# Two encoder layers on one core: host-laid input and modulation weights, first shift and scale by TensorE tile by tile

## What is computed

```python
def adaln(c, w, b):
    mod = (c @ w + b)[:, None, :]
    shift, scale, gate = jnp.split(mod, 3, axis=-1)
    return shift, scale, gate

for l in range(DEPTH):
    shift, scale, gate = adaln(c, w_ada_mix[l], b_ada_mix[l])
    u = x * (1.0 + scale) + shift
    y = hybrid_mixer(u, w_in[l], ...)
    x = layer_norm(DN_ALPHA * x + (1.0 + gate) * y, ln1_g[l], ln1_b[l])
    shift, scale, gate = adaln(c, w_ada_ffn[l], b_ada_ffn[l])
    u = x * (1.0 + scale) + shift
    y = conv_gated_mlp(u, w_up[l], ...)
    x = layer_norm(DN_ALPHA * x + (1.0 + gate) * y, ln2_g[l], ln2_b[l])
```

## Time and profile before

| what | value |
| --- | --- |
| median of 3 runs | 2102.32 us (2102.18 to 2103.11) |
| the profiled execution's own time | 2101.31 us |
| its span, first to last instruction | 2099.5 us |
| mean granted TensorE clock | 0.997 |
| busy share of PE, DVE, ACT, POOL | 98%, 57%, 49%, 67% |
| HBM read, written | 242.71 MB, 4.26 MB |

### The profile page before, as it was taken

One profiled execution on the slowest core, in us unless ns is written; L12 is line 12 of the kernel. 1 busy time (PEld: TensorE's weight loads), 2 busy tenths in 40 slices (PEclk: granted clock), 3 DMA queues, 4 the chain that ended last, 5 costly groups with the idle time before them and its releaser, 6 DMA issues.

```text
span 2099.5 us, 27374 instructions
## 1 busy us (share of the span) xinstructions
PE 2064.8 (98%) x9619; PEld 1701.8 (81%) x9619; DVE 1191.1 (57%) x1940; ACT 1031.2 (49%) x1845; POOL 1413.6 (67%) x1780
## 2 busy tenths in 40 slices
PE   7999999999999999999999999999999999999997
PEld 6877778787888878888788888888878888888887
DVE  5888888675515554777632645587651455332235
ACT  3585356555516674374643756235562465333332
POOL 4987767755778887875557885564556776545454
PEclk9999999999999999999999999999999999999999
DMA  8644544533434354553233333332323332434332
GB/s 301 157 134 148 161 127 148 162 108 103 121 111 124 107 162 145 141 159 93 76 100 106 111 111 91 101 103 73 100 76 107 88 104 84 128 99 123 94 100 78
DMA packets 421510, 250.07 MB, mean 119 GB/s; under 512 B 48149, under 2 KB 393085, under 8 KB 421373
## 3 DMA queue, kind: packets, MB, share of 16 engines
q1 hardware_dynamic: 420506, 248.03, 39.8%
q10 hardware_dynamic: 867, 0.29, 0.1%
HBM read 242.71 MB, written 4.26 MB: 118 GB/s over the span
## 4 chain that ended last, share of the span: by engine, by line
PE 86%; POOL 5%; ACT 3%; DVE 3%; issue 2%; ACTq 0%; DMA 0%; POOLq 0%; DVEq 0%
PE fg L886 27%; PE fg L888 27%; PE fg L887 27%; POOL w_lo L1932 3%; PE bank_s L984 1%; POOL ada_acc L2003 1%; ACT ada L1324 1%; PE bank_l L915 1%; PE bank_t L993 1%; PE bank_t L1006 1%; DVE bank_c L1539 0%; POOL ssum L2030 0%; POOL u_lo L2012 0%; ACT probs L1291 0%; ACT probs L1283 0%
## 5 line engine op out<-in xcount | busy, mean ns | idle before, releaser
L1932 POOL TENSOR_TENSOR w_lo<-raw,w_hi 128x256 fp32r<-128x256 f32 (+1 forms) x1425 | 1031.3, 755 | 609.8 <-ACT w_hi L1163 608.7
L886 PE MATMUL fg<-u_hi,w_hi 128*128 128x512 f32 x2112 | 834.7, 395 | 6.2 <-DVE u_lo L1519 2.6
L888 PE MATMUL fg<-u_hi,w_lo 128*128 128x512 f32 x2112 | 823.7, 390 | 0.0
L887 PE MATMUL fg<-u_lo,w_hi 128*128 128x512 f32 x2112 | 823.5, 390 | 0.0
L1163 ACT ACTIVATE w_hi<-raw 128x1024 fp32r<-128x1024 f32 (+2 forms) x387 | 375.6, 971 | 385.6 <-PE fg L888 278.4
L886 PEld LDWEIGHTS fg<-u_hi,w_hi 128*128 128x128 f32 x2112 | 397.1, 188 | 102.5 <-issue 14.5
L888 PEld LDWEIGHTS fg<-u_hi,w_lo 128*128 128x128 f32 x2112 | 397.0, 188 | 84.2
L887 PEld LDWEIGHTS fg<-u_lo,w_hi 128*128 128x128 f32 x2112 | 397.4, 188 | 80.1 <-issue 0.5
L1539 DVE SCALAR_TENSOR_TENSOR bank_c<-glu,par,bank_c 128x512 f32<-128x512 f32 x448 | 306.1, 747 | 0.1
L1886 DVE SCALAR_TENSOR_TENSOR x<-fg,mod,x 128x512 f32<-128x512 f32 (+1 forms) x168 | 121.6, 724 | 319.3 <-PE fg L888 319.0
L888 PE MATMUL fg<-h_hi,w_lo 128*128 128x512 f32 (+1 forms) x704 | 269.8, 383 | 0.0
(11 more groups left out here) (272 smaller groups left out, 1860.8 us busy)
## 6 DMA issues: line engine op xcount, KB each, us to landing
raw<-in_w_up_dram SPq DMA_DIRECT2D x176, 512.0 KB, 3.8
ada<-in_w_ada_ffn_dram SPq DMA_DIRECT2D x48, 512.0 KB, 4.4
raw<-in_w_down_dram SPq DMA_DIRECT2D x64, 384.0 KB, 3.5
raw<-in_w_in_dram SPq DMA_DIRECT2D x40, 512.0 KB, 4.0
raw<-in_w_down_dram SPq DMA_DIRECT2D x64, 320.0 KB, 3.1
ada<-in_w_ada_mix_dram SPq DMA_DIRECT2D x32, 512.0 KB, 4.2
raw<-in_w_in_dram SPq DMA_DIRECT2D x32, 256.0 KB, 3.7
raw<-in_w_out_dram SPq DMA_DIRECT2D x32, 256.0 KB, 2.9
```

Of the source, the lines that this page charges most:

```text
L886: pe.matmul(out, hi[:, k, :], rhi, start=k == order[0], stop=False)
L887: pe.matmul(out, hi[:, k, :], rlo, start=False, stop=False)
L888: ins = pe.matmul(out, lo[:, k, :], rhi, start=False, stop=k == order[-1])
L1932: ins = pool.tensor_tensor(lo_of(n)[:, ks, :], raw[n % NRAW][:, ks, :], hi_of(n)[:, ks, :].bitcast(F32), ALU.subtract)
```

## The change

The host now lays out three inputs. x is handed over with features in rows, so SP loads its tiles directly into `x` (`load_x(b, i)`, 512 KB for two tiles of one block). The first modulation weights come as eight blocks of 1 MB (`ada_first`): block k has what shift and scale of feature tile k need, with the output features on the partitions' axis of the weights of a TensorE product. The later modulation weights come transposed (`ada_t`), one output feature a row. The first half of the output is stored with features in rows, and the host turns it.

On TensorE, `first_part(k)` makes shift and scale of tile k with 16 products that have a single moving column (`ccol`). Parts 0 and 1 stand ahead of the first product of slab pair 0 and 1, and part k+1 ahead of the pair's tile k for k = 1 to 6. VectorE adds the constants (`first_fold_in`), ScalarE makes u and `u_hi` (`first_inputs`, for all eight tiles), and VectorE `u_lo` (`first_lo`). The products of the identity (`idle_products`) are gone. The transposes of the convolution taps (`taps_turn`) move behind the pair's last tile. c is spread over the partitions once (`c_rows`, two products of one row by 512 columns).

Later sums: GpSimd multiplies a quarter (128 output features x 1024) by `c_rows` (`ada_weigh`), and ScalarE, one slab later, sums each row by a copy with an accumulated output (steps "ae", `ada_total`); for chunks 8 to 10 VectorE does both in one instruction. The steps "as" and "xt" are gone from all engines, and "tm" is now only a place in SP's list.

```diff
-        if c in ONES_CHUNKS:
-            at(ns[-1] + 2, "as", c)
-        else:
-            put(ns[-1] + 2, "as", c)
+        for part, n in enumerate(ns):
+            if c not in DVE_CHUNKS:
+                at(n + 1, "ae", c, part)
+        if c >= DVE_CHUNKS[0]:
+            used[ns[-1] + 2] += 7
     for n, what, i in ((18, "gate", 0), (47, "gate", 1), (100, "ss", 2), (145, "gate", 2), (165, "ss", 3),
...
+            def load_x(b, i):
+                sp.dma_start(x[:, 2 * i:2 * i + 2, b * T:(b + 1) * T],
+                             a["x"][2 * i * P:2 * (i + 1) * P, b * T:(b + 1) * T].rearrange("(k p) n -> p k n", p=P)).then_inc(in_x[b][i], 16)
             def load_first(k):
-                c0, c1, k0, k1, i, slot = FIRST_PIECES[k]
-                dst = first_ada[i][:].rearrange("p a n -> p (a n)")[:, slot * T:slot * T + (k1 - k0) * (c1 - c0)]
-                sp.dma_start(dst.rearrange("p (k n) -> p k n", n=c1 - c0),
-                             a["w_ada_mix"][0, k0 * P:k1 * P, c0:c1].rearrange("(k p) n -> p k n", p=P)).then_inc(in_first[k], 16)
+                for half in (0, 1):
+                    sp.dma_start(first_ada[k][:, half, :], a["ada_first"][k, half]).then_inc(in_first[k][half], 16)
             def load_ada(m):
-                c, part = CHUNKS_BEFORE + m // QUARTERS, m % QUARTERS
-                l, ffn, j = c // NCHUNK // 2, c // NCHUNK % 2, c % NCHUNK
                 if m >= 2:
-                    sp.wait_ge(ada_add[added(m - 2)[0]], added(m - 2)[1])
-                src = a["w_ada_ffn" if ffn else "w_ada_mix"][l, part * 2 * P:(part + 1) * 2 * P, j * T:(j + 1) * T]
-                sp.dma_start(ada[m % 2][:], src.rearrange("(k p) n -> p k n", p=P)).then_inc(in_ada[m % 2], 16)
+                    sp.wait_ge(*part_done(m - 2))
+                sp.dma_start(ada[m % 2][:], a["ada_t"][m * P:(m + 1) * P, :].rearrange("p (h n) -> p h n", h=2)).then_inc(in_ada[m % 2], 16)
...
+            for k in range(DT):
+                load_first(k)
+                if k < 2:
+                    load_x(0, k)
+                    load_w(k)
+                if k == 3 or k == 5:
+                    load_x(0, (k + 1) // 2)
+            load_rows(rows2, rows3)
             for n in range(2, NRAW):
                 load_w(n)
-            sp.wait_ge(in_first[-1], 16)
-            load_rows(rows2, rows3)
             sp.dma_start(nsink[:], a["sinks"]).then_inc(in_sinks, 16)
-            for t in range(TB, TT):
-                load_x(t)
+            for i in range(DT // 2):
+                load_x(1, i)
...
+            def first_part(k):
+                if k >= 2:
+                    pe.wait_ge(first_fold, 2 * (k - 1))
                 for half in (0, 1):
+                    pe.wait_ge(in_first[k][half], 16)
+                    for d in range(DT):
+                        ins = pe.matmul(bank_c[k % 2][:, half:half + 1], first_ada[k][:, half, d * P:(d + 1) * P], ccol[:, d:d + 1],
+                                        start=(half, d) == (0, 0), stop=(half, d) == (1, DT - 1))
+                ins.then_inc(first_sum, 1)
...
+                if ns[0] == 0:
+                    first_part(1)
...
+                    if ns[0] == 0 and 0 < k < DT - 1:
+                        first_part(k + 1)
...
-                    if ns[0] == 0 and k == DT // 2 - 1:
-                        first_rest()
+                    if ns[0] == 0 and k == DT - 1:
+                        taps_turn()
...
+            for half in (0, 1):
+                pe.matmul((bank_t, bank_s)[half][:], ones_1[0:1, :], c_rows[0:1, half, :], start=True, stop=True).then_inc(set_pe, 1)
             pe.wait_ge(in_const, 16 * IN_CONST)
             for l in range(DEPTH):
                 ins = pe.transpose(fg[1][:, l * P:l * P + N1], rows1[0:N1, l, :], ident[0:N1, 0:N1])
             ins.then_inc(set_pe, 1)
-            first_sums(0)
-            idle_products(12, fg[0])
+            pe.wait_ge(in_ccol, 16)
+            first_part(0)
...
             def first_inputs(k):
-                if k % (DT // 2) == 0:
-                    act.wait_ge(fold_step, FOLDED["half", 2 * k // DT])
-                if k == 0:
-                    for half in (0, 1):
-                        act.wait_ge(x_evac[half], TB)
+                act.wait_ge(first_fold, 2 * k + 2)
+                if k % 2 == 0:
+                    act.wait_ge(in_x[0][k // 2], 16)
+                if k >= 2:
+                    act.wait_ge(ilo[0], k - 1)
+                inputs(tmp[:, k % 2, :], xs(0, k), 0, k, iu)
                 inputs(u_hi[0][:, k, :], xs(0, k), 0, k, ihi)
-                if k < DT // 2:
-                    if k >= 2:
-                        act.wait_ge(ilo, k - 1)
-                    inputs(tmp[:, k % 2, :], xs(0, k), 0, k, iu)
...
-            def ada_scale(c, part):
+            def ada_total(c, part):
                 m = (c - CHUNKS_BEFORE) * QUARTERS + part
-                act.wait_ge(in_ada[m % 2], 16 * (m // 2 + 1))
-                for i in (0, 1):
-                    k = 2 * part + i
-                    act.activation(ada[m % 2][:, i, :], ada[m % 2][:, i, :], ACT.Copy, scale=ccol[:, k:k + 1]).then_inc(ada_mul, 1)
-            def stage(t, src):
+                act.wait_ge(ada_mul, 2 * sum(ada_engine(i) == "act" for i in range(m + 1)))
+                rows = ada[m % 2][:].rearrange("p h n -> p (h n)")
+                act.activation(rows, rows, ACT.Copy, accum_out=total_of(c, part)).then_inc(ada_done["act"], 1)
...
+            for half in (0, 1):
+                act.wait_ge(set_pe, half + 1)
+                act.activation(c_rows[:, half, :], (bank_t, bank_s)[half][:], ACT.Copy).then_inc(set_col, 1)
+            act.wait_ge(set_pe, 3)
             act.activation(par1[:], fg[1][:].rearrange("p (l n) -> p l n", n=P)[:, 0:DEPTH, 0:N1], ACT.Copy).then_inc(set_par, 1)
+            split_hi(0)
             for k in range(DT):
-                if k == DT // 2:
-                    split_hi(2)
                 first_inputs(k)
-            act.wait_ge(set_pe, 4)
+                if k == 0:
+                    split_hi(1)
+            split_hi(2)
+            act.wait_ge(set_pe, 5)
...
+            def first_fold_in(k):
+                dve.wait_ge(first_sum, k + 1)
+                o = OFF["b_ada_mix"] + k
+                sums = bank_c[k % 2]
+                dve.tensor_tensor(bias[:, 0, k:k + 1], sums[:, 0:1], par1[:, 0, o:o + 1], ALU.add).then_inc(first_fold, 1)
+                dve.scalar_tensor_tensor(out=gain[:, 0, k:k + 1], in0=sums[:, 1:2], scalar=1.0, in1=par1[:, 0, o + DT:o + DT + 1],
+                                         op0=ALU.add, op1=ALU.add).then_inc(first_fold, 1)
+            def first_lo(k):
+                dve.wait_ge(ihi, k + 1)
+                dve.wait_ge(iu, k + 1)
+                dve.tensor_tensor(u_lo[0][:, k, :], tmp[:, k % 2, :], u_hi[0][:, k, :].bitcast(F32), ALU.subtract).then_inc(ilo[0], 1)
...
+            def ada_total(c, part):
...
+                rows = ada[m % 2][:].rearrange("p h n -> p (h n)")
+                dve.scalar_tensor_tensor(out=rows, in0=rows, scalar=1.0, in1=c_rows[:].rearrange("p h n -> p (h n)"),
+                                         op0=ALU.mult, op1=ALU.mult, accum_out=total_of(c, part)).then_inc(ada_done["dve"], 1)
...
+            dve.wait_ge(set_par, 1)
+            first_fold_in(0)
+            for k in range(DT):
+                if k + 1 < DT:
+                    first_fold_in(k + 1)
+                first_lo(k)
...
+            def ada_weigh(c, part):
                 m = (c - CHUNKS_BEFORE) * QUARTERS + part
+                pool.wait_ge(in_ada[m % 2], 16 * (m // 2 + 1))
+                pool.wait_ge(set_col, 2)
+                for i in (0, 1):
+                    pool.tensor_tensor(ada[m % 2][:, i, :], ada[m % 2][:, i, :], c_rows[:, i, :], ALU.mult).then_inc(ada_mul, 1)
...
-            for n in range(2):
-                split_lo(n)
-            for k in range(DT // 2):
-                first_lo(k)
+            split_lo(0)
+            split_lo(1)
             angles(0)
             split_lo(2)
-            pool.wait_ge(set_pe, 4)
+            angles(1)
+            pool.wait_ge(set_pe, 5)
...
+def first_rows(w):
+    return np.ascontiguousarray(w[:, :2 * D].reshape(DT, P, 2, DT, P).transpose(3, 2, 1, 0, 4).reshape(DT, 2, P, D))
+def ada_rows(w_mix, w_ffn):
+    rows = np.concatenate([w[l].T for l in range(DEPTH) for w in (w_mix, w_ffn)])
+    return np.ascontiguousarray(rows[CHUNKS_BEFORE * T:])
...
+            "x": np.ascontiguousarray(inputs["x"][0].T), "ada_first": first_rows(inputs["w_ada_mix"][0]),
+            "ccol": np.ascontiguousarray(inputs["c"][0].reshape(DT, P).T),
+            "ada_t": ada_rows(inputs["w_ada_mix"], inputs["w_ada_ffn"])}
     for name in _INS + [n for n in made if n not in _INS]:
```

350 lines of the change are left out of this document (66 added, 284 removed).

## The result

The changed kernel takes **2160.44 us** (median of 4 runs, 2158.70 to 2165.72), beside 2102.72 us for the kernel before in the same session: the ratio is 1.0276, with a 95% interval of 1.0255 to 1.0296. The sign was forecast, the size was not: 2125 us was forecast with a range up to 2142. The profiled execution is the longest of the four, 2165.72 us with a span of 2163.9 us.

A forecast was written before the change was run, and what follows sets the result against it. TensorE was taken as the bound over most of the run, with GpSimd setting the pace from 51.4 to 137 us. Start +32.3 less 10 got gave +22.3 on 2101.31, 2123.6, plus 1.0 for the median: 2125 us, range 2103 to 2142.

The forecast's parts named there:

- 32.3 and -10: Forecast terms: slab 2 starts 32.3 us late, and TensorE's shorter list behind the start gives back 10 us.
- The start's mechanism: Before slab 2: two parts precede the pair, each tile waits for `u_lo`, and single-column records run mostly at low clock.
- the low-clock column of the working: Start worked out at low clock throughout: a period of 10.7 us, slab 2's first products at 98.4 us.
- 8.0 us a period, between 6.1 and 10.7: Start, one part and one tile: most tiles' products bring the clock back for part of the next single-column stretch.
- The rival with low clock throughout: Start: the clock stays low, slab 2 is 49.5 us late, +39.5 us in all, 2142 us; chance 0.20.
- Single columns cost the same at either clock: Start: a part always takes 3.3 us, slab 2 at about 73 us, 2114 us; chance 0.15.
- Got: 10 us: Behind the start: of 16.1 us taken off TensorE's list, 10 us shortens the time, with ends 5 and 16.
- What lies between 51 and 137 us: Second stretch: 4.8 us off TensorE's list is not got, since GpSimd sets the pace there.
- the wait for `kz`: TensorE's wait for VectorE's `kz` ahead of the first attention scores, forecast at 5 to 8 us.
- Cheap edits ... All at nothing: Later sums on ScalarE and VectorE, SP's later wait and the output tail: hidden, cost put at nothing.
- The chain I named for the case that the cover went: Second stretch: SP's wait for ScalarE's sum would hold raw weights and rotary swaps, costing what it lasts.
- The case of a clock that stays up: Start: single-column weight loads hold the clock, start 11 us late, 2103 or 2097 us in all; chance 0.17.

The follow-up runs named there:

- e4_one_mul: The changed kernel with one GpSimd multiplication of 1024 columns in place of two of 512; 2152.10 us.
- e5: The changed kernel with 20 products of the identity ahead of part 0 and 6 ahead of each half part; 2158.17 us.
- e1_pool_wait: The changed kernel with GpSimd waiting for the first of a quarter's two multiplications before issuing the second; 2141.11 us.
- v3: The changed kernel with the start of the kernel before and a GpSimd wait between its two multiplications; 2092.17 us.
- e6_dense_lo_first: The changed kernel with identity products ahead of parts, `u_lo` ahead of the next tile's constants, and GpSimd's wait between multiplications; 2129.77 us.

## Why the prediction was right or wrong

Against the profiled execution before: 2101.3 + 44.2 (slab 2) + 19.2 (slab 2 to 350) + 1.0 (the tail) = 2165.7 us. The prediction had 32.3 and -10.

- **The start's mechanism** was right: no product of the pair until two parts are done, a wait for `u_lo` ahead of every tile, low clock in the single-column parts. By the low-clock column of the working slab 2 was to start its products at 98.4; it did at 95.6. Part 3 to 7 take 6.8 us for 6.6, the tile 2.7 for 2.6, the wait 0.92 for 1.4, the period 10.46 for 10.7. Part 0 began at 13.9 us and not at 11.5, since the last parameter row landed later.
- **The mis-sized term** there was "8.0 us a period, between 6.1 and 10.7". I took it that a tile's 2.6 us of products bring the pace back for a part of the next; in the changed kernel they did so once in six, and in e4_one_mul, whose start is the same, never (slab 2 at 97.79 us). The period measured 10.46 us, and the term is 11.9 us too small (44.2 for 32.3). The rival with low clock throughout, at 0.20, was the true one.
- **"Single columns cost the same at either clock"** falls: 0.107 us in e5, 0.213 in the changed kernel. The Trainium skill, "TensorE: Matmul & The Clock Gate", section "LDWEIGHTS (loading the stationary operand)", gives a load as its columns divided by 1.2; for 128 columns that is an estimate of 107 ns, the fast figure. At the slow pace the records stand twice as far apart, which that rule doesn't say.
- **"Got: 10 us"**, with 5 and 16 as ends: 6.1 us in e1_pool_wait. Its parts were right where TensorE sets the pace: "tm" gave 3.6 us for 3.2, a sum by transposes about 0.4. What lies between 51 and 137 us was rightly called not got, but the loss there was larger than the gain (v3: from -6.5 us at slab 7 to +0.7 at slab 12). GpSimd is busy 39.77 of 41.40 us in the changed kernel's stretch; the wait for `kz`, 1.77 us before and forecast at 5 to 8, is 5.2, and 4.3 in e1_pool_wait, without the starved instruction.
- **The failing step** was "Cheap edits ... All at nothing", and in it what GpSimd's two multiplications are. I counted them as an operation of 1.3 us more per chunk and asked who waits for them. I did not ask what else changes when two instructions that waited for each other no longer do. That cost 19.3 us by the medians, 25.5 between the profiles of the changed kernel and of e1_pool_wait at slab 350. With the 11.9 us of the start, 3.9 less got than forecast and 1.0 in the tail it makes the 42 us between the forecast for the profiled execution and its time. The chain I named for the case that the cover went (SP's wait holds raw weights and rotary swaps) was the one that ran, but VectorE started it, not ScalarE's sum.
- The case of a clock that stays up (0.17) was wrong: the changed kernel ran 64 single-column records without a pause at 0.21 us each. The fast pace held throughout only in e6_dense_lo_first, with 12 wide records ahead of each 16 thin ones and no wait for `u_lo`.

## What to carry to other kernels

When an edit removes a wait between two GpSimd instructions, read VectorE's longest instructions, not its mean: three in 1903 cost 25 us in the profiled execution here (19 by the medians), and one wait put back took it off again. A sum by single-column products belongs where TensorE would be idle; put on its path in this kernel, it cost its records at the slow pace, and the products beside it ran at that pace too.
